# The expert bias of a hybrid encoder layer: its fp32r matmuls rewritten on bf16 operands

## The reference

```
def expert_block(args):
    e, tok, gt = args
    xb = xf[tok]
    gu = xb @ w_gu[e] + b_gu[e]
    gate, up = gu[:, :D_EXPERT], gu[:, D_EXPERT:]
    gate = jnp.minimum(gate, SWIGLU_LIMIT)
    up = jnp.clip(up, -SWIGLU_LIMIT, SWIGLU_LIMIT)
    h = (up + 1.0) * gate * jax.nn.sigmoid(SWIGLU_ALPHA * gate)
    y = h @ w_down[e] + b_down[e]
    return y * gt[:, None].astype(y.dtype)
```

## Time and profile before

| | |
|---|---|
| three runs | 2473.07, 2474.29, 2476.85 us (median 2474.29) |
| profiled execution | 2473.07 us, its span 2471.3 us |
| mean granted clock of PE | 0.963 |
| busy | PE 92%, PEld 68%, DVE 72%, ACT 57%, POOL 12% |
| DMA | 489.28 MB, mean 198 GB/s |

### The profile page before, as it was taken

How to read it: one execution, slowest core, us unless ns; L and a number is a source line. 1 busy time by engine, 2 the same in 40 slices (tenths; PEclk the granted TensorE clock), 3 DMA queues, 4 the chain that set the end, 5 groups by cost and what they waited for, 6 DMA issues and landing times.

```text
span 2471.3 us, 37393 instructions
## 1 busy us (share of the span) xinstructions
PE 2281.1 (92%) x10580; PEld 1677.8 (68%) x10581; DVE 1771.8 (72%) x3318; ACT 1412.0 (57%) x2108; POOL 286.6 (12%) x224
## 2 busy tenths in 40 slices
PE   8999998789997599999999999999999999999992
PEld 3544448468654288877777877878787787787872
DVE  0486785446335567787987889787978978878797
ACT  0368624555221255576766667565757757656575
POOL 0001931100010001110011011010101101111010
PEclk9999998799998599999999999999999999999996
DMA  4100002000204366786997889786978978868794
GB/s 170 69 5 34 1 17 103 0 1 1 94 1 151 148 202 221 226 299 227 357 320 237 282 288 341 272 290 216 354 255 294 358 248 300 296 223 290 233 311 183
DMA packets 80493, 489.28 MB, mean 198 GB/s; under 512 B 12147, under 2 KB 13427, under 8 KB 29331
## 3 DMA queue, kind: packets, MB, share of 16 engines
q1 hardware_dynamic: 67024, 450.06, 50.7%
q0 software_dynamic: 11440, 34.10, 6.2%
q10 hardware_dynamic: 1974, 4.43, 0.5%
HBM read 462.32 MB, written 33.69 MB: 201 GB/s over the span
## 4 chain that ended last, share of the span: by engine, by line
PE 70%; DVE 15%; issue 7%; ACT 3%; DVEq 2%; DMA 1%; ACTq 0%; POOL 0%; POOLq 0%; SPq 0%
PE ps L812 8%; PE ps L810 8%; PE ps L811 8%; DVE wlo L1627 8%; PE ps L538 6%; PE ps L807 6%; PE ps L808 6%; PE ps L549 5%; PE ps L730 5%; PE ps L831 4%; PE ps L712 2%; DVEq L382 2%; PE ps L693 1%; PE ps L700 1%; PE ps L579 1%
## 5 line engine op out<-in xcount | busy, mean ns | idle before, releaser
L1627 DVE TENSOR_TENSOR wlo<-raw,whi 128x1024 fp32r<-128x1024 f32 x776 | 931.0, 1220 | 189.2 <-ACT whi L1103 147.8
L1103 ACT ACTIVATE whi<-raw 128x1024 fp32r<-128x1024 f32 x776 | 817.7, 1060 | 375.8 <-PE ps L812 346.7
L811 PE MATMUL ps<-wlo,xhi 128*128 128x512 f32 x1024 | 400.2, 391 | 0.0
L812 PE MATMUL ps<-whi,xlo 128*128 128x512 f32 x1024 | 400.1, 391 | 0.0
L810 PE MATMUL ps<-whi,xhi 128*128 128x512 f32 x1024 | 400.1, 391 | 0.0
L812 PEld LDWEIGHTS ps<-whi,xlo 128*128 128x128 f32 x1024 | 193.0, 188 | 40.7
L811 PEld LDWEIGHTS ps<-wlo,xhi 128*128 128x128 f32 x1024 | 193.0, 188 | 40.4
L810 PEld LDWEIGHTS ps<-whi,xhi 128*128 128x128 f32 x1024 | 193.0, 188 | 38.5
L810 PE MATMUL ps<-whi,hhi 128*128 128x512 f32 x512 | 210.1, 410 | 0.0
L812 PE MATMUL ps<-whi,hlo 128*128 128x512 f32 x512 | 201.2, 393 | 0.0
L811 PE MATMUL ps<-wlo,hhi 128*128 128x512 f32 x512 | 200.2, 391 | 0.0
(11 more groups left out here) (343 smaller groups left out, 3349.4 us busy)
## 6 DMA issues: line engine op xcount, KB each, us to landing
raw<-in_w_gu SPq DMA_DIRECT2D x260, 1024.0 KB, 5.3
raw<-in_w_dn SPq DMA_DIRECT2D x128, 1024.0 KB, 5.1
raw<-in_w_out SPq DMA_DIRECT2D x2, 2048.0 KB, 13.6
h1all<-in_x SPq DMA_DIRECT2D x4, 1024.0 KB, 8.4
hext<-h1all SPq DMA_DIRECT2D x8, 512.0 KB, 12.0
acc<-accst SPq DMA_DIRECT2D x8, 512.0 KB, 2.6
fin<-acc SPq DMA_DIRECT2D x4, 1024.0 KB, 8.3
out<-fin SPq DMA_DIRECT2D x8, 512.0 KB, 2.6
```

What stands on the lines that cost most here:

```text
L811: pe.matmul(bank_ap, hi, wlo[:, slot, col, :], start=False, stop=False)
L812: return pe.matmul(bank_ap, lo, whi[:, slot, col, :], start=False, stop=stop)
L1103: act.activation(whi[:, j % 2, 2 * g:2 * g + 2, :], raw[:, (j + 2) % 3, 2 * g:2 * g + 2, :], ACT.Copy)\
L1627: dve.tensor_tensor(wlo[:, j % 2, s, :], raw[:, (j + 2) % 3, s, :], whi[:, j % 2, s, :].bitcast(f32), ALU.subtract).then_inc(lo_done, 1)
```

## The change

The three bias pieces become bf16 instead of fp32r, in SBUF and in DRAM. `brow` shrinks to its three used rows, so its zeroing on ACT goes. The bias matmul contracts over 3 partitions with bf16 operands: `brow`, and ones taken from an existing constant (`cb`, whose first 128 columns are all ones) for block 0 or a new tile `tail_ones` for the tail. All three roundings move from ACT to POOL, which now makes the pieces alone. Three DVE instructions that wrote `bias_ones` become two memsets.

```diff
--- before.py
+++ after.py
@@ -237,11 +237,11 @@
         ysb = at("ysb", X + 80.5, [P, 2, D])
         slots = at("slots", X + 88.5, [P, NT, 2 * P], bf16)
         slot_iota = at("slot_iota", 57.25, [P, CAP], bf16)
-        bias_ones = at("bias_ones", 58.25, [P, 2, P], f32r)
+        tail_ones = at("tail_ones", 57.75, [P, P], bf16)
         gu = at("gu", X + 92.5, [P, 2, SLAB])
-        brow = at("brow", X + 134.5, [P, 2 * D], f32r)
+        brow = at("brow", X + 134.5, [3, 2 * D], bf16)
         bsrc = at("bsrc", X + 102, [NE, 2 * D])
-        bpart = at("bpart", X + 110, [NE, 3, 2 * D], f32r)
+        bpart = at("bpart", X + 110, [NE, 3, 2 * D], bf16)
         relv = at("relv", 62, [P, NT])
         act_tmp = at("act_tmp", 62.6, [P, 1])
         slot_n = at("slot_n", 62.05, [P, 2, 3])
@@ -261,7 +261,7 @@
 
         ps = [ctx.enter_context(nc.psum_tensor(f"ps{n}", [P, 512], f32)) for n in range(8)]
         hext = nc.dram_tensor("hext", [S, HROW], f32, kind="Internal").ap()
-        bias3 = nc.dram_tensor("bias3", [NE, 3, 2 * D], f32, kind="Internal").ap()
+        bias3 = nc.dram_tensor("bias3", [NE, 3, 2 * D], bf16, kind="Internal").ap()
         acc = nc.dram_tensor("acc", [S, D], f32, kind="Internal").ap()
 
         ident = consts[:, C_ID:C_ID + P]
@@ -362,7 +362,6 @@
         act_table = sem("act_table")
         sum_kept = sem("sum_kept")
         bias_all_in, bias_step, bias_out = sem("bias_all_in"), sem("bias_step"), sem("bias_out")
-        bias_rounded, brow_zero = sem("bias_rounded"), sem("brow_zero")
         tokens_in = sem("tokens_in")
         pool_passed = sem("pool_passed")
         xg_set, all_added = sem("xg_set"), sem("all_added")
@@ -470,8 +469,8 @@
             for t in range(NT):
                 sp.wait_ge(h1_done, t + 1)
                 sp.dma_start(hext[t * P:(t + 1) * P, 0:D], h1all[:, t, :]).then_inc(h_out, 16)
-            sp.wait_ge(bias_rounded, 3)
-            sp.dma_start(bias3, bpart[:, :, :].bitcast(f32)).then_inc(bias_out, 16)
+            sp.wait_ge(bias_step, 6)
+            sp.dma_start(bias3, bpart[:, :, :]).then_inc(bias_out, 16)
             sp.wait_ge(gates_done, 1)
             sp.dma_start(hext[:, D:HROW].rearrange("(t p) e -> p t e", p=P), gates[:, :, :]).then_inc(gate_out, 16)
             for t in range(NT):
@@ -838,7 +837,8 @@
                     bank_n, uses = gu_place(b, j, i, n1, blocks)
                     pe.wait_ge(gu_read[bank_n], since(uses))
                     pe.wait_ge(bgu_in, i * 16 + 16)
-                    pe.matmul(ps[bank_n][:, :], bias_ones[:, b, :], brow[:, j * SLAB:(j + 1) * SLAB], start=True, stop=False)
+                    ones = tail_ones[0:3, :] if b else cb[0:3, 0:P]
+                    pe.matmul(ps[bank_n][:, :], ones, brow[:, j * SLAB:(j + 1) * SLAB], start=True, stop=False)
                     for k in range(KT):
                         if k % 2 == 0 and b == blocks[0]:
                             if j == 0:
@@ -902,7 +902,7 @@
             pe.wait_ge(tokens_in, 1)
             for pair in range(4):
                 turn(xg, (1, 0), pair, (2, 1, 3, 2)[pair], first=pair == 1)
-            pe.wait_ge(tail_const, 6)
+            pe.wait_ge(tail_const, 5)
             with pe.Fori(0, n_items) as i:
                 b1, n1 = entry(1, i, 1), entry(2, i, MAX_ITEMS)
                 with pe.If(b1 > 0):
@@ -1072,9 +1072,6 @@
                     turned(t - 1)
                 if t > 1:
                     router_out(t - 2)
-                if 1 <= t <= 3:
-                    act.wait_ge(bias_step, t)
-                    act.activation(bpart[:, t - 1, :], bsrc[:, :], ACT.Copy).then_inc(bias_rounded, 1)
             turned(NT - 1)
             router_out(NT - 2)
             router_out(NT - 1)
@@ -1091,7 +1088,7 @@
 
             def biases(e):
 
-                act.dma_start(brow[0:3, :].bitcast(f32), bias3[bass.ds(e, 1), :, :].rearrange("o s c -> (o s) c")).then_inc(bgu_in, 16)
+                act.dma_start(brow[:, :], bias3[bass.ds(e, 1), :, :].rearrange("o s c -> (o s) c")).then_inc(bgu_in, 16)
 
             def take_hi(j, pieces, i=0):
 
@@ -1170,12 +1167,9 @@
 
             starts(act, y_done[0:1])
             act.activation(act_tmp[:, :], consts[:, C_COL:C_COL + 1], ACT.Silu).then_inc(act_table, 1)
-            for n in range(2):
-                act.activation(brow[:, n * D:(n + 1) * D], consts[:, 0:D], ACT.Copy, scale=0.0).then_inc(brow_zero, 1)
             act.wait_ge(act_table, 1)
-            act.wait_ge(brow_zero, 2)
             act.wait_ge(bias_out, 16)
-            act.dma_start(brow[0:3, :].bitcast(f32), bias3[0, :, :]).then_inc(bgu_in, 16)
+            act.dma_start(brow[:, :], bias3[0, :, :]).then_inc(bgu_in, 16)
             for b in range(NB):
                 act.wait_ge(out_of[b], len([1 for v in PLACE.values() if v[0] == b]))
             take_hi(0, range(4))
@@ -1724,9 +1718,8 @@
             for t in range(NT):
                 dve.tensor_scalar(slots[:, t, 0:CAP], slot_iota[:, :], relv[:, t:t + 1], None, ALU.is_equal)\
                    .then_inc(slots_done, 1)
-            dve.tensor_copy(bias_ones[:, 0, :], onesf).then_inc(tail_const, 1)
-            dve.tensor_copy(bias_ones[:, 1, 0:TAIL], onesf[:, 0:TAIL]).then_inc(tail_const, 1)
-            dve.tensor_scalar(bias_ones[:, 1, TAIL:P], onesf[:, TAIL:P], 0.0, None, ALU.mult).then_inc(tail_const, 1)
+            dve.memset(tail_ones[:, 0:TAIL], 1.0).then_inc(tail_const, 1)
+            dve.memset(tail_ones[:, TAIL:P], 0.0).then_inc(tail_const, 1)
             dve.memset(hb[TAIL:P, 1, :], 0.0).then_inc(tail_const, 1)
             find_index(1, 2, 0)
             take_lo(0, range(4))
@@ -1807,9 +1800,10 @@
             bs = serial(pool, bias_step)
             up_bias = bsrc[:, :].rearrange("p (j s c) -> p j s c", j=4, s=2)[:, :, 1, :]
             bs(pool.tensor_scalar(up_bias, up_bias, 1.0, None, ALU.add))
-            for k in range(2):
-                pool.wait_ge(bias_rounded, k + 1)
-                bs(pool.tensor_tensor(bsrc[:, :], bsrc[:, :], bpart[:, k, :].bitcast(f32), ALU.subtract))
+            for k in range(3):
+                bs(pool.tensor_copy(bpart[:, k, :], bsrc[:, :]))
+                if k < 2:
+                    bs(pool.tensor_tensor(bsrc[:, :], bsrc[:, :], bpart[:, k, :], ALU.subtract))
 
             for n in range(2):
                 pool.wait_ge(acc_out[n], 8 * NT)
```

## The result

The changed kernel takes 2505.31 us (median of 4 runs) against 2474.66 us: slower, ratio 1.0129 with a 95% interval of 1.0116 to 1.0140. The forecast was 2470.3 us, the range ended at 2477.0. Its profiled execution took 2506.74 us.

The account below looks back on a forecast made before the run. PE was taken to bound two-block items, DVE to cover one-block items. Gains of 3.1 + 0.1 (first item at half clock) + 0.3 + 0.4, say 4 us, off 2474.3 gave 2470.3 us; range 2465.5 to 2477.

Parts of the forecast that it names:

- the one on rows: Bias matmuls in the loop: contracting over 3 rows instead of 128 costs nothing, since 512 columns still stream.
- Rival C: Loop: fp32r weights can't load beside a bf16 matmul; 0.11 to 0.19 us at 125 crossings, 2484 to 2494 us; chance 0.12.
- The sign of B: After transposes in the loop: the step from bias matmul to its successor stays at 0.31 us.
- The exposed bias matmuls: Two-block items, after slot matmuls and twice after transposes: shorter bf16 load saves 0.08 us each, 3.1 us in all.
- The five covered bias matmuls: Two-block items, behind full fp32r products: load hidden, streaming gains 0.005 us each, 0.3 us in all, bounds 0 and 0.65.
- The fourfold rate: Weight loads: fast load four times faster in theory, about twice as measured; the trace's 0.11 to 0.03 us agrees with theory.
- rival B: Loop: no gain in PE, exposed 0.11 us is fixed whatever the type; only 0.4 us ahead stays, 2473.9 us; chance 0.20.
- One-block items at nothing: 19 one-block items, 57 exposed bias matmuls: gain taken as 0, because DVE works without a gap through the quarters.
- The 21 crossings of the chain: One-block items: places where the chain of waits crosses a bias matmul; if all real, 0.08 us each, 1.7 us.
- Ahead of the loop: Before the row gather: two memsets replacing three DVE writes of bias_ones take 0.4 us off, between 0.1 and 0.6.
- Making the pieces at nothing: Before the loop: moving casts from ACT to POOL is worth 0; POOL done by about 681 us, store only at 781.90.

Follow-up runs that it names:

- e6: Changed kernel plus a second 3-row matmul, with zero weights, directly behind each bias matmul: 2530.76 us, ratio 1.0226.
- e2: Kernel before with only its fp32r bias matmul cut to three rows: 2517.57 us against 2475.57, ratio 1.0167.
- e1: Changed kernel with its bf16 bias matmul over all 128 rows again, brow zeroed by ACT: 2475.52 us against 2475.57 for the kernel before, ratio 0.9999.
- e3: Kernel before with POOL instead of ACT rounding the pieces, still to fp32r: 2475.16 us against 2475.57, ratio 0.9998.
- e7: Kernel before with the bias matmul of the tail blocks left out: 2464.08 us against 2474.91, ratio 0.9955.

## Why the prediction was wrong

**The step that failed** is the one on rows: "That the matmul contracts over 3 rows instead of 128 I cost at nothing: the stream still has 512 columns." The stream does, and it stayed at 0.22 us (e6). What it left out is the neighbours: for them the overlap of weight load and matmul goes, on both sides. Cutting the rows alone, with the old type, costs 42 us (e2); giving them back, with the new type, costs nothing (e1). The term put at nothing should have been 8 x 0.295 us (2.36 us per item) x 13 = 30.7 us.

**A row of before showed it, and I did not read it.** The mLSTM stage has matmuls over 32 rows (L629) between others over 128 (L623, L635). Its timeline in the kernel before:

```profile
396.44 0.97 PEld L623 LDWEIGHTS ps<-w_m,ucT 128*128 128x128 f32 x8
397.54 0.96 PEld L629 LDWEIGHTS ps<-g_ng,consts 32*128 32x128 f32 x8
397.54 1.15 PE L629 MATMUL ps<-g_ng,consts 32*128 32x128 f32 x8
398.62 0.97 PEld L635 LDWEIGHTS ps<-mqk 128*128 128x128 f32 x8
398.62 1.16 PE L635 MATMUL ps<-mqk 128*128 128x128 f32 x8
399.51 0.64 PEld L641 LDWEIGHTS ps<-mC,mqk 128*128 128x128 f32 x5
```

At both changes of height the loads pause: they end at 397.41 and 398.50, and go on only at 397.54 and 398.62, in the same hundredth as the first matmul of the new height. No load crosses the edge. At the next hand-over, to L641, the height stays at 128 and there is no pause (398.62 + 0.97 = 399.59, L641 loads from 399.51). Within a group one load starts 0.11 us after another, across either edge 0.31 us, so an edge takes 0.20 us more here, and it does so in all eight passes of that stage. Two such edges would be 0.4 us, an estimate from small matmuls and above the 0.29 measured, but enough to give the 3 rows a rival of their own. I had looked only at the loop's own fp32r to bf16 edge, which is of whole height on both sides. The Trainium skill has it as well ("TensorEngine Tiling (Array Packing)", section "Key Properties"): a change of the tiling mode, not of the tile alone, drains the engine. Its modes have 128, 64 or 32 rows (section "Available Configurations"). The runs agree for whole against 3 and 64 rows, with the step between 64 and 65; whether 32 against 64 drains, no run here shows. What I cited in its place from the Trainium skill ("TensorE: Matmul & The Clock Gate", section "LDWEIGHTS (loading the stationary operand)"), that a load goes by columns and not by rows, is true of the load alone: in bf16 it is drawn at 0.09 us for 3 rows and at 0.10 for 97 or 128.

**Rival C** named the right direction, with the wrong cause and one edge instead of two: it forecast 0.11 to 0.19 us at 125 crossings. There are 0.295 us at the 104 crossings in two-block items. Its sign came true: the product starts 0.31 us after the bias matmul in mid-stream, and its 0.11 us are exposed. Even so C is not right: its own condition, the mixed type, is in e1 without a loss, and its range ended at 2494 us, 11 us short. The sign could not tell the causes apart, since the change altered type and rows at once. The sign of B, 0.31 us after transposes, came true as well, for a matmul that drains.

**The exposed bias matmuls** (0.08 us x 39): at whole height the saving is 0.02 us after transposes and 0.11 after slot matmuls (e1). The rate of sixteen bf16 loads in a row wasn't the price of one bf16 load behind an fp32 transpose. The five covered bias matmuls of an item, forecast to gain 0.005 us each, cost 0.01 to 0.02 us more. (The fourfold rate that the prediction takes from the Trainium skill stands there for fp8; the 0.08 us doesn't rest on it.) Whole-height bf16 came out within noise of no change in three kernels (0.9999, 0.9993, 0.9995), so rival B's picture, no gain in PE, fits the type best; a gain under the 0.1% or so of these intervals isn't excluded.

**One-block items at nothing**: right, and shown more harshly than planned. PE is busy 1 us more in them and they hardly grew (39.22 against 39.21 us; 1.5 us over all, and 1.0 us in e3, where the loop is unchanged). DVE without a gap was the right row to read. The 21 crossings of the chain there would have cost 21 x 0.295 = 6.2 us, had they been real.

**Ahead of the loop** 0.28 us against 0.4 forecast. The first bias matmul still comes 0.8 us later (865.05 for 864.28). The stages before, which the change doesn't touch, ran 1.4 us later in this execution (POOL's first bias step at 653.89 for 652.50).

**Making the pieces at nothing**: right (e3). A cast was priced at up to 5.5 us and took 1.88.

**The rest.** Counted on the starts of one two-block item, five covered bias matmuls at 0.29, two after transposes at 0.28 and one after slots at 0.17 (0.97 us from the first slot matmul to the second product before, 1.14 now) make 2.2 of the 2.36 us. What is left, under 0.2 us, was not followed up.

## What to carry to other kernels

A small matmul is priced with its two neighbours. Before cutting the contraction to the rows that hold data, look at what height the matmuls beside it have: 65, 97 and 128 rows stood beside whole ones at no cost, 3 and 64 rows cost 0.28 to 0.29 us on a stream that starts every 0.23. If such matmuls can't be padded, put them next to each other: between two of 3 rows there was no edge (e6). And where PE is the bound, a covered matmul costs its full stream, 0.22 us for an fp32r one (e7) and 0.23 for a bf16 one over 3 rows (e6): taking it off PE is what pays.

## What the runs showed of the hardware

- The height at which a bf16 matmul beside fp32r ones of 128 rows counts as whole lies between 64 and 65 rows: item 63.03 us against 60.54.
- At an edge neither the load of the small matmul nor that of the next one is pulled ahead (1105.45 and 1105.77, each with its own matmul); between two 3-row matmuls it is (load at 1112.07, matmul at 1112.28, 0.22 us between starts).
- fp32r beside bf16 at whole height drains nothing: the fp32r load starts with the bf16 matmul (1107.65). The bf16 load is drawn 0.23 us after the fp32r matmul ahead of it began (1107.42), where an fp32r load is drawn with it (1023.22 and 1023.21); three starts take 0.70 us all the same, against 0.68.
